# Chunk mask as twelve rows of the MLA score contraction, and the maximum negated as it is taken

## The reference, cut

```
q_chunk = (q0 + arange(Q_BLOCK)) // 64
k_chunk = arange(q1) // 64
s = (q_nope @ k_nope^T + q_rope @ k_rope^T) * scale
s = where(k_chunk[None, :] <= q_chunk[:, None], s, -inf)
out = softmax(s) @ v          # 16 heads, 64 + 32 score dims, 64 value dims
```

## Time and profile before

| | us |
|---|---|
| median of 3 runs (2280.11 to 2282.62) | 2282.21 |
| span of the profiled execution | 2284.0 |
| PE busy in it | 2128.9 (93%) |
| DVE busy | 1125.8 (49%) |
| POOL busy | 1105.4 (48%) |
| ACT busy | 671.8 (29%) |

### The profile page before, as it was taken

How to read it: one execution, slowest core, us unless ns; L and a number is a source line. 1 busy time by engine, 2 the same in 40 slices (tenths; PEclk the granted TensorE clock), 3 DMA queues, 4 the chain that set the end, 5 groups by cost and what they waited for, 6 DMA issues and landing times.

```text
span 2284.0 us, 27160 instructions
## 1 busy us (share of the span) xinstructions
PE 2128.9 (93%) x9840; PEld 1691.4 (74%) x9840; DVE 1125.8 (49%) x1213; ACT 671.8 (29%) x1069; POOL 1105.4 (48%) x657
## 2 busy tenths in 40 slices
PE   5999999988999999999999998998999999989996
PEld 3777776877778878788878876886776777668774
DVE  6545653737541211212111287215777777754576
ACT  3334444221121000000001132114555555560322
POOL 1635554522833634633444383334656666653373
PEclk9999998997999999999999998998999999989998
DMA  3100000112211211211111131110000000001122
GB/s 139 48 19 20 14 14 19 46 38 92 92 46 53 67 55 46 74 46 54 57 55 46 55 101 37 46 46 28 20 19 19 19 19 19 19 28 46 46 69 97
DMA packets 31624, 106.98 MB, mean 47 GB/s; under 512 B 3440, under 2 KB 3632, under 8 KB 31568
## 3 DMA queue, kind: packets, MB, share of 16 engines
q1 hardware_dynamic: 27520, 96.53, 12.7%
q10 hardware_dynamic: 4048, 9.67, 1.2%
HBM read 101.83 MB, written 4.26 MB: 46 GB/s over the span
## 4 chain that ended last, share of the span: by engine, by line
PE 59%; POOL 15%; issue 14%; DVE 8%; ACT 2%; ACTq 0%; POOLq 0%; DMA 0%; DVEq 0%
PE ps L220 45%; POOL probs_lo L677 11%; PE ps L385 4%; PE ps L249 3%; PE ps L237 2%; POOL w_lo L1921 2%; POOL w_hi L1919 2%; DVE h_lo L366 1%; DVE tmp L1747 1%; DVE x L1749 1%; DVE S_all L1287 1%; DVE tmp L362 1%; DVE result L1753 0%; PE ps L1594 0%; DVE ssq L413 0%
## 5 line engine op out<-in xcount | busy, mean ns | idle before, releaser
L1919 POOL TENSOR_TENSOR w_hi<-w_raw,zero 128x1024 fp32r<-128x1024 f32 (+1 forms) x173 | 334.7, 1935 | 816.0 <-PE ps L220 575.7
L1921 POOL TENSOR_TENSOR w_lo<-w_raw,w_hi 128x1024 fp32r<-128x1024 f32 (+1 forms) x173 | 433.0, 2503 | 13.6
L220 PE MATMUL ps<-h_hi,w_lo 128*128 128x512 f32 x1328 | 338.4, 398 | 5.6 <-DVE x L512 5.1
L220 PE MATMUL ps<-h_hi,w_hi 128*128 128x512 f32 x1328 | 328.0, 389 | 0.0
L677 POOL TENSOR_TENSOR probs_lo<-probs,mla_p_hi 128x512 fp32r<-128x512 f32 x192 | 220.3, 1167 | 182.0 <-ACT probs L670 181.9
L220 PE MATMUL ps<-h_lo,w_hi 128*128 128x512 f32 x1216 | 302.0, 391 | 0.0
L220 PEld LDWEIGHTS ps<-h_hi,w_lo 128*128 128x128 f32 x1328 | 251.2, 191 | 61.6 <-issue 10.0
L220 PEld LDWEIGHTS ps<-h_hi,w_hi 128*128 128x128 f32 x1328 | 249.3, 188 | 51.7
L220 PEld LDWEIGHTS ps<-h_lo,w_hi 128*128 128x128 f32 x1216 | 230.0, 189 | 48.4
L1369 DVE TENSOR_TENSOR tmp<-ps,tmp 128x1024 f32<-128x1024 f32 x22 | 26.9, 1224 | 370.3 <-PE ps L220 363.6
L712 DVE TENSOR_REDUCE mx<-ps 128x1 f32<-128x256 f32 (+1 forms) x192 | 144.5, 785 | 78.5 <-PE ps L655 77.8
(11 more groups left out here) (345 smaller groups left out, 3911.7 us busy)
## 6 DMA issues: line engine op xcount, KB each, us to landing
w_raw<-in_wpack SPq DMA_DIRECT2D x173, 512.0 KB, 3.3
x<-in_xT ACTq DMA_DIRECT2D x16, 512.0 KB, 8.3
out<-result SPq DMA_DIRECT2D x8, 512.0 KB, 2.9
p_raw<-in_pT ACTq DMA_DIRECT2D x1, 1024.0 KB, 7.2
const_stage<-in_consts SPq DMA_DIRECT2D x1, 788.0 KB, 4.4
pos_i<-in_pos SPq DMA_DIRECT2D x1, 512.0 KB, 6.4
vec<-in_vecs SPq DMA_DIRECT2D x1, 284.0 KB, 5.3
mla_q_hi<-c_neg ACTq DMA_DIRECT2D x16, 4.0 KB
```

What stands on the lines that cost most here:

```text
L220: last = nc.tensor.matmul(dst[:, half, :], w[slot][:, kt, :], a[:, i, t], start=(n == 0), stop=(n == total - 1))
L1919: nc.gpsimd.tensor_tensor(w_hi[s][:, kts, :], raw[s][:, kts, :], no_change[:, kts, :], ALU.add).then_inc(w_hi_done, 1)
L1921: nc.gpsimd.tensor_tensor(w_lo[s][:, kts, :], raw[s][:, kts, :], w_hi[s][:, kts, :].bitcast(F32), ALU.subtract)\
```

## The change

In MLA the mask becomes part of the contraction. Twelve rows, 96 to 107, are added to `q_hi` and `k_hi`. For each of eight blocks j of 128 positions one row is 1 at the queries of its first chunk and -1e30 at the keys of its second; for blocks 0, 2, 4 and 6 another row is 1 at the block's queries and -1e30 at the keys of the next block. The high by high score matmul contracts over 109 rows (the twelve, and the row maximum, which moves to row 108), the two with a low part over 96 instead of 97, and the maxima over 108 instead of 96. The mask matmuls of MLA go: 8 on line 612 and 8 on line 655 for each of 16 heads. Fox keeps its own.

The rows come from a new input of 13 x 2048 values, loaded once by a DMA on ACT's queue during MLA's gate projection, and are copied by POOL in `mla_constants_pool`. PE now waits for six of these constants before the maxima of head 0. The negation on line 717 goes in both attentions: `reduce_max` is called with `negate=True`, and the transpose of `mx` waits for the eight maxima themselves. The table of masks in the constants is halved.

```diff
@@ score_pe @@
-            r = slice(0, A.rows)
+            r, r_low = slice(0, A.rows), slice(0, A.rows_low)
-            masked = d >= 0
-            nc.tensor.matmul(out, k_lo[b][r, keys], q_hi[b][r, t], start=True, stop=False)
-            nc.tensor.matmul(out, k_hi[b][r, keys], q_lo[b][r, t], start=False, stop=False)
+            masked = d >= 0 and A.mask is not None
+            nc.tensor.matmul(out, k_lo[b][r_low, keys], q_hi[b][r_low, t], start=True, stop=False)
+            nc.tensor.matmul(out, k_hi[b][r_low, keys], q_lo[b][r_low, t], start=False, stop=False)
@@ max_pe @@
-            nc.tensor.matmul(PS[:, bank + c, 0:w], queries, k_hi[b][r, c * HALF:c * HALF + w], start=True, stop=False)
-            nc.tensor.matmul(PS[:, bank + c, d:w], ident_bf[:, :], masks[:, A.mask, 0:w - d], start=False, stop=True)\
-                .then_inc(A.mp_ready, 1)
+            last = nc.tensor.matmul(PS[:, bank + c, 0:w], queries, k_hi[b][r, c * HALF:c * HALF + w], start=True, stop=A.mask is None)
+            if A.mask is not None:
+                last = nc.tensor.matmul(PS[:, bank + c, d:w], ident_bf[:, :], masks[:, A.mask, 0:w - d], start=False, stop=True)
+            last.then_inc(A.mp_ready, 1)
@@ max_row_pe @@
-            pe.wait_ge(A.mx_done, n + 1)
+            pe.wait_ge(A.max_done, (n + 1) * N_MAX)
@@ max_dve, negate_dve @@
-                                 PS[:, bank, 0:max_width(i)[1]], AX_X).then_inc(A.max_done, 1)
-
-        def negate_dve(dve, A, n):
-            dve.wait_ge(A.max_done, (n + 1) * N_MAX)
-            nc.vector.tensor_scalar(mx[:, 0:8], mx[:, 0:8], -1.0, None, ALU.mult).then_inc(A.mx_done, 1)
+                                 PS[:, bank, 0:max_width(i)[1]], AX_X, negate=True).then_inc(A.max_done, 1)
@@ step_pe @@
-                if isinstance(n, int) and n == 1 and A is mla:
-                    pe.wait_ge(mla_constants, 8)
...
                     elif prev is None:
                         pe.wait_ge(A.setup, 4)
+                        pe.wait_ge(mla_constants, 6)
@@ mla_in_act @@
+                if i == 1:
+                    act.dma_start(mask_stage[MASK_ROWS, :], mask_rows).then_inc(mask_in, 16)
@@ mla_constants_pool @@
+            pool.wait_ge(mask_in, 16)
...
-                for dst, value in ((q_lo[b][96:97, :], 0.0), (k_hi[b][96:97, :], 1.0), (k_lo[b][96:97, :], 0.0), (vaug[b][:, :, HD:P], 1.0)):
-                    nc.gpsimd.memset(dst.bitcast(F32), value).then_inc(mla_constants, 1)
+                for dst, src in ((q_hi, slice(0, T)), (k_hi, slice(T, 2 * T))):
+                    nc.gpsimd.tensor_copy(dst[b][MASK_ROWS, :], mask_stage[MASK_ROWS, src]).then_inc(mla_constants, 1)
...
+                nc.gpsimd.memset(vaug[b][:, :, HD:P].bitcast(F32), 1.0).then_inc(mla_constants, 1)
@@ new function @@
+def score_mask_rows():
+    t = np.arange(T)
+    q, k = np.zeros((N_MASK_ROWS + 1, T), np.float32), np.zeros((N_MASK_ROWS + 1, T), np.float32)
+    for j in range(DT):
+        q[j] = t // CHUNK == 2 * j
+        k[j] = (t // CHUNK == 2 * j + 1) * NEG
+    for i, b in enumerate(PAST_BLOCKS):
+        q[DT + i] = t // P == b
+        k[DT + i] = (t // P == b + 1) * NEG
+    k[N_MASK_ROWS] = 1.0
+    return np.concatenate([q, k], axis=1)
```

More of the change, by code:

```diff
@@ L97 @@
 K_MASK = 384
-K_ATT = K_MASK + 4 * 256
+K_ATT = K_MASK + 2 * 256
 K_CNT = K_ATT + 128
@@ L101, with build @@
 N_CONST = K_CNT + 40
-def build(nc, wpack, xT, pT, vecs, consts, pos, outT, f_rows):
+PAST_BLOCKS = (0, 2, 4, 6)
+N_MASK_ROWS = DT + len(PAST_BLOCKS)
+MASK_ROW0 = NOPE + ROPE
+def build(nc, wpack, xT, pT, vecs, consts, pos, mask_rows, outT, f_rows):
     with ExitStack() as ctx:
@@ L149, in build @@
         ident_bf = const("ident_bf", [P, P], BF16)
-        masks = const("masks", [P, 4, 256], BF16)
+        masks = const("masks", [P, 2, 256], BF16)
         att_mask = const("att_mask", [P, P], U32)
@@ L525, in build, with __init__ @@
         class Attention:
-            def __init__(self, k, heads, rows_max, rows, mask):
-                self.k, self.heads, self.rows_max, self.rows, self.mask = k, heads, rows_max, rows, mask
+            def __init__(self, k, heads, rows_low, rows_max, rows, mask):
+                self.k, self.heads, self.mask = k, heads, mask
+                self.rows_low, self.rows_max, self.rows = rows_low, rows_max, rows
                 self.s_ready = sem(f"{k}_s_ready")
@@ L549, in __init__ @@
                 self.norm_done = sem(f"{k}_norm_done")
-                self.mx_done = sem(f"{k}_mx_done")
                 self.setup = sem(f"{k}_setup")
@@ L733, in max_row_act @@
             act.dma_start(A.bufs[0][b][A.rows - 1:A.rows, :].bitcast(F32), c_neg[:, :].bitcast(F32)).then_inc(A.row_in[b], 16)
-        fox = Attention("fox", FOX_H, HD + 1, HD + 2, 0)
+        fox = Attention("fox", FOX_H, HD + 2, HD + 1, HD + 2, 0)
         fox.bufs, fox.v_lo, fox.p_hi = buffers("fox", R_X, R_X + 24576, R_S + 8192, R_S + 20480, R_S + 24576)
@@ L738, in build @@
         fox_vT = at("fox_vT", R_S + 16384, [HD, T])
-        mla = Attention("mla", MLA_H, NOPE + ROPE, NOPE + ROPE + 1, 2)
+        mla = Attention("mla", MLA_H, MASK_ROW0, MASK_ROW0 + N_MASK_ROWS, MASK_ROW0 + N_MASK_ROWS + 1, None)
         mla.bufs, mla.v_lo, mla.p_hi = buffers("mla", R_H + 40960, R_S + 8192, R_S + 16384, R_S + 24576, R_S + 4096)
@@ L832, in step_dve @@
                     norm_half_dve(dve, A, prev, 1 - b, 0, tile, gate)
-            negate_dve(dve, A, n)
             vaug_dve(dve, A, n, b)
@@ L1631, in mla_constants_pool @@
             pool.wait_ge(w_split, U_HEAD + 1 + 2)
+            pool.wait_ge(mask_in, 16)
             n = 0
             for b in range(2):
-                for dst, value in ((q_lo[b][96:97, :], 0.0), (k_hi[b][96:97, :], 1.0), (k_lo[b][96:97, :], 0.0), (vaug[b][:, :, HD:P], 1.0)):
-                    nc.gpsimd.memset(dst.bitcast(F32), value).then_inc(mla_constants, 1)
+                for dst, src in ((q_hi, slice(0, T)), (k_hi, slice(T, 2 * T))):
+                    nc.gpsimd.tensor_copy(dst[b][MASK_ROWS, :], mask_stage[MASK_ROWS, src]).then_inc(mla_constants, 1)
                     n += 1
                     pool.wait_ge(mla_constants, n)
-        mla_constants = sem("mla_constants")
+                nc.gpsimd.memset(vaug[b][:, :, HD:P].bitcast(F32), 1.0).then_inc(mla_constants, 1)
+                n += 1
+                pool.wait_ge(mla_constants, n)
+        mla_constants, mask_in = sem("mla_constants"), sem("mask_in")
+        MASK_ROWS = slice(MASK_ROW0, MASK_ROW0 + N_MASK_ROWS + 1)
+        mask_stage = at("mask_stage", R_W + 8192, [P, 2 * T])
         def mla_prepare_act(act, n, b, turn):
@@ L1772, in setup_dve @@
             for dst, k, n in ((ident[:, :], K_ID, P), (ones[:, :], K_ONE, P), (head_mean[:, :], K_BLK, P),
-                              (ident_bf[:, :], K_ID, P), (masks[:, :, :].rearrange("p a n -> p (a n)"), K_MASK, 1024),
+                              (ident_bf[:, :], K_ID, P), (masks[:, :, :].rearrange("p a n -> p (a n)"), K_MASK, 512),
                               (att_mask[:, :], K_ATT, P), (small_const[:, :], K_CNT, 40)):
@@ L2066, in shape_constants @@
     later = i[None, :] > i[:, None]
[L2067 to L2072, removed]
+    by_query = c[:, K_MASK:K_MASK + 256]
+    by_query[:, 0:P], by_query[:, P:] = later * NEG, NEG
+    by_key = c[:, K_MASK + 256:K_MASK + 512]
+    by_key[:, 0:P], by_key[:, P:] = NEG, later.T * NEG
     c[:, K_ATT:K_ATT + P] = (i[:, None] // CHUNK == i[None, :] // CHUNK) & (i[:, None] <= i[None, :])
@@ L2174 @@
         "pos": np.ascontiguousarray(np.broadcast_to(np.asarray(inputs["positions_2"]), (P, T))),
+        "mask_rows": score_mask_rows(),
     }
```

## The result

The changed kernel takes 2256.09 us, the median of 4 runs (2255.05 to 2258.9); the kernel before took 2282.41 in the same session. The ratio is 0.9882, 95% interval 0.9865 to 0.99: 26.3 us less, where 32 were forecast.

The account below looks back on a forecast made before the run. PE was nearest its limit, with ACT, DVE and PE binding by turns in a head and the negation waiting for POOL. -13.5 - 1.0 - 10.5 - 4.5 + 0.7 - 3 = -31.8 us from 2284.0; median 2250, range 2238 to 2266.

Parts of the forecast that it names:

- rival (A): Masks give less: first half, piece 3's wait is really for POOL's piece 1, 7 us less; chance 0.20, shared.
- The masks' term, 13.5 us: MLA: removing the mask matmuls gains 0.9 us a head, over fifteen heads that attend while another is prepared.
- I take 0.5 us for this third: First third of an MLA head: four score masks gone shorten ACT's wait before piece 3, gaining 0.5 us.
- The 0.55 for maximum 4: Middle of an MLA head, where DVE binds: 0.5 us from ACT and up to 0.07 from masks.
- The last step, 0.35: End of an MLA head, where PE binds again: three masks (row blocks 6 and 7, piece 11) give 0.35 us.
- the head of 26.9 us: Sign that the forecast is right: MLA period of 26.9 us a head where it was 28.5.
- The negation, 10.5 and 4.5 us: Head's end: without the negation's wait for POOL, 14 x 0.75 us in MLA, 4.5 us in fox.
- Nothing new waits: After the negation goes at an MLA head's end, the earlier work that follows makes no engine newly wait.
- The clock, 3 us: Heads' ends: less PE idle removes some clock falls, 2.1 us each; between 0 and -12, taken as -3 us.
- rival (B): More gain: clock no longer falls (-9 us more), ACT gives 0.3 us more a head (-4.5): 2237; chance 0.12.
- Rival (C): Slower: longer wait before row block 6 lowers the clock in every head, 2282 to 2325 us; chance 0.08.
- Head 0, +0.7 us: Head 0: DVE's chain may meet POOL's row copies; between 0 and 4 us lost, taken as +0.7.

Follow-up runs that it names:

- e2: Changed kernel with the negation put back as its own instruction, mask rows kept: 2281.9 us, ratio 1.0003 to the kernel before.
- e5: e1 (mask matmuls kept) plus rotary sum and normalization each reading one operand from PSUM: 2238.9 us, ratio 0.9808.
- e4: Changed kernel with rotary sum and normalization each reading one operand from PSUM instead of two from SBUF: 2225.2 us, ratio 0.9749.
- e1: Kernel before with only the negation moved into reduce_max, all mask matmuls kept: 2260.6 us, ratio 0.9905.
- e7: Mask rows alone (e2, negation kept) plus four unused matmuls in PE's idle time at a head's end: 2267.6 us, ratio 0.9934.
- e6: Kernel before plus four unused matmuls at a head's end: 2275.5 and 2274.3 us; two more executions took 3497 and 3493 us.
- e8: e4 with DVE taking maximum 4 before normalizing the old head's first half: 2224.0 us.

## Why the prediction was right, and where it was not

The total was right to 6 us (2250 against 2256.1), but that is in part luck: two errors of opposite sign. For the rows with their copies the forecast had 13.5 + 1.0 - 0.7 = 13.8 us, and they gave 4.5. For the clock it had 3, and 9.5 came. What is left of the 26.3 us, 12.3, is the negation's, for which it had 15.

**What bounds.** Right for the middle of a head (DVE) and its end (the negation). For the first third ACT was named, and the wait before piece 3 put down to the mask. Behind the mask stood POOL's piece 1, itself held up by DVE's rotary sum already in the kernel before (1.70 us for its first subtraction): with the mask gone, 0.32 of the 0.46 us stay (e2). That was the first half of rival (A).

**A mask matmul costs 0.125 us of PE.** Right: in the changed kernel the scores follow each other at the spacing of unmasked ones, and where PE binds (e5 against e4) the sixteen are worth 0.80 us a head, with 0.9 forecast for the same path.

**The masks' term, 13.5 us.** Wrong in size. They gave 4.5 us (e1 against the changed kernel), 0.37 us a head. The step that failed is "I take 0.5 us for this third": it gave 0.17 alone (e7) and 0.05 beside the flag (12.79 against 12.84). The 0.55 for maximum 4 rested on it and fell with it, to 0.23 and 0.11. The last step, 0.35, came to 0.26. The wait at line 658 was forecast at 1.5 us and is 1.4, but without the gain in front of it. Of the signs named, the head of 26.9 us did not come (27.69), nor the earlier maximum 4: counted from the transpose it is 0.24 us later (22.42 against 22.18).

**The negation, 10.5 and 4.5 us.** Its size at the head's end was right, 0.77 us against 0.75 in MLA and 0.82 in fox. "Nothing new waits" was wrong: with DVE's end of a head 0.5 us earlier, its reciprocal step falls under `w_lo` (1.24 us instead of 0.73) and the sum behind `probs_lo`. That took 0.34 us of the 0.77 back. On the other side, every second head, at the turn of the loop, had been 0.52 us longer than its neighbour and is now 0.13 longer; this came with the flag alone (28.20 against 28.07), and not with the filling (28.50 against 28.00). Why the turn costs less when PE does not wait ahead of it was not tried. The flag on the reduction costs nothing that the trace shows: `reduce_max` has the same minimum and maximum as before, 0.41 and 1.22 us.

**The clock, 3 us.** Much too small: six falls are gone, three in MLA and three in fox, 9.5 us in all, over a third of the gain. Each costs 1.6 us. The forecast read 2.1, because it took the long period of 30.60 against a neighbour of 28.48, while the heads at the turn of the loop, where all three falls lie, take 29.0 without one. It had the mechanism and took a third of it; this is the first half of rival (B), which priced it at 12. Rival (C) had the other direction of it, at the wrong place: a wait of 1.4 us before row block 6 left the clock alone in all fourteen heads, and it was the head's end, with the negation kept (e2), where seven heads fell.

**Head 0, +0.7 us.** DVE's chain met POOL's copies, and at its end POOL's next split. POOL, DVE, then PE's first maximum:

```profile
1547.38 2.05 POOL L1639 CAST mla_q_hi<-mask_stage 13x1024 fp32r<-13x1024 f32 x1 [14.37 <-DVE ckv_lo L1558]
1549.49 1.92 POOL L1639 CAST mla_k_hi<-mask_stage 13x1024 fp32r<-13x1024 f32 x1
1547.30 3.20 DVE L1626 TENSOR_TENSOR mla_k_lo<-k_rope,mla_k_hi 32x1024 fp32r<-32x1024 f32 x2
1556.67 2.13 DVE L1687 TENSOR_TENSOR mla_q_lo<-rope_x,mla_q_hi 32x1024 fp32r<-32x1024 f32 x1
1558.86 1.54 PE L660 MATMUL ps<-mla_k_hi,mla_q_hi 108*128 108x256 f32 x4 [8.92 <-DVE mla_q_lo L1687]
```

A copy of 13 rows takes up to 2.05 us where DVE is beside it; the two instructions on `k_lo` take 3.20 us together, where they took 2.35, and the last one, beside `w_hi`, 2.13 instead of 1.48. PE starts 0.06 us behind that, so the new wait for the constants cost nothing, as forecast. (Its printed wait is 8.92 us instead of 4.99 because its projection was done earlier beside DVE's chain: before, nearly half of it ran at the low clock, with 0.43 us from start to start instead of 0.23.) From the first `k_lo` to PE's first maximum it is 11.56 us now and was 10.33: +1.2 us, where 0.7 was taken. From there to the transpose it is 8.27 us instead of 9.33, the 1.0 us that the forecast gave head 0 and the last head together. The last head's attention ended 0.5 us sooner, of which half is left at the end (268.2 against 268.5).

**Contraction over 109 rows.** Right: 512 columns step at 0.23 us with 96, 108 and 109 rows.

## What to carry to other kernels

A step moved earlier on an engine takes its port conflicts along: look up which instructions of VectorE with two SBUF inputs the move brings beside GpSimd, on both sides, since the lock cost in either order here (0.54 and 0.83 us a head). Writing one operand to PSUM in place took it away with the same number of arithmetic instructions, and that was worth 31 us here, more than the change itself (26). And price the clock at a place where PE idles as an event with a count, so many falls of so many microseconds: work taken off PE can be given back whole, as the rows alone showed (2281.9 against 2281.5 before).

## What was not expected of the hardware

Four matmuls of no use in the idle time at a head's end made a kernel 14 us faster (2281.9 to 2267.6), the granted clock in the MLA loop going from 0.97 to 1.00. It is no safe recipe yet, with two executions of e6 unexplained. A GpSimd subtraction and a VectorE sum that start 0.14 us apart cost both: the sum 1.0 us, and the subtraction behind, 1.98 us instead of 1.02, as much again. And the kernel of e4 (e8 is as fast), with the flag, the mask rows and no VectorE instruction of the attention loop's normalization or rotary sum that reads SBUF twice, runs in 2225.2 us, 0.9749 of the kernel before.
